# Two-layer hybrid attention, linear attention and MoE step: alternating level banks with output one head later, five more ada units on VectorE, a longer busy opening

## The chip, the cores and the metric

The kernel runs on one core of a Trainium2 chip. The metric is device time in microseconds of one execution. All data is float32. The engines that matter are PE (TensorE, matrix products), DVE (VectorE), ACT (ScalarE), POOL (GpSimd) and SP, which only issues DMAs.

## The reference

A step has two layers with the same structure. It handles two sequences of 128 tokens (s = 0: context, s = 1: latent tokens) of width 1024. Cut to what matters here:

```python
mod = silu(cond) @ w_ada + b_ada             # 6 x 1024 values per sequence: sh1, sc1, g1, sh2, sc2, g2
h = rmsnorm(x, norm1) * (1 + sc1) + sh1
q, k, v, gq, gk, gv, gg, lr_f, lr_b, ga, gb = split(h @ w_in)
o_attn = softmax(q k^T) v                    # 8 heads, 2 kv heads
o_gla, s_f, s_b = bidirectional_gla(gq, gk, gv, la_f, la_b, s0_f, s0_b)    # 4 heads
o_gla = rmsnorm(o_gla, gla_norm) * silu(gg)
merged = sigmoid(ga) * (o_attn @ w_pa) + sigmoid(gb) * (o_gla @ w_pb)
x = x + g1 * (merged @ w_out)
h2 = rmsnorm(x, norm2) * (1 + sc2) + sh2
x = x + g2 * grouped_moe(h2, ...)            # 16 experts, the best group of 4, top 2 in it
```

## The kernel before

**Weights.** All dense weights come through `ring`, six slots of 2 MB. `dense_order()` writes their order out by hand, and SP loads unit n when unit n - 6 has been used (`used(n)` names the semaphore). A unit is a piece of `w_ada` (12 per layer, `ada[0]` to `ada[11]`, 512 columns each), of `w_in` (five projections, then four of the gates ga and gb), `w_pa`, `w_pb` or one of two of `w_out`. After them the expert weights use the same slots, and three more (`more`, `mixer`).

**An ada unit** gives 4 x 128 values of `mod` for both sequences, in one of two ways. On PE: `ada_a` (L543, 8 products, 16 records in the trace) into bank 7, an ACT copy to the front half of `wide`, `ada_b` (L552, 4 transposes into bank 6), and two small DVE operations (`ada_bias`, L1456 and L1457). On DVE (`ada_blocks`, L1471): four blocks of two `SCALAR_TENSOR_TENSOR` over 1024 elements, one for each sequence, which read the ring slot and `cs_rows` (the silu of the condition in every partition) and write a throwaway product over all of `wide`. Before, units 4 to 7 of layer 0 go the second way (`VECTOR_ADA`), all others the first. The blocks stand at fixed places of DVE's program: 4 before the QK norm, 4 inside it, 2 before and 5 after the copy of gk, 1 after the first softmax. `cs_rows` is written by a POOL DMA from `cs_dram`, and lies over `qe`, `ke` and the front of `lpar` (the GLA state), which for this reason is loaded when the vector units are done.

**Opening** (layer 0). PE runs `WARM` products on zeros, then the first ada unit, the norm sum, ada unit 2, and half of the input projection (`first_half`, L667) while the other halves of the weights are still on their way; then ada units 1 and 3, and `second_half` (L676).

**Fills.** From the attention on, PE, ACT and DVE each call `fill(l)` at the same places of their programs; each call takes one entry of `fill_list(l)`: one of eight gate chunks (L563, 16 products), an ada unit, one of four `pa` chunks (L576, o_attn times w_pa, 8 products), or `HOLE`, nothing. The attention takes entries 0 to 6, all gates, to give PE work while DVE and ACT make the softmax (L1598 to L1604). The eighth gate and all else are taken in the linear attention, two entries a head. An ada unit that PE took is finished (`ada_b`, `ada_bias`) at the next fill. With the first `pa` entry ACT makes the sigmoids of the gates (L1124 to L1126, a table load before and after).

**Linear attention (GLA).** Head i of 8 (4 heads times 2 sequences) goes through: `gla_in` (PE L801, L807: decays into banks 0 and 1), the exponential (ACT L1232) into one of two halves of `ereg`, `qe` (DVE L1616) and `ke` (POOL L1948), `gla_levels` (PE L822, 8 products into banks 2 and 3), mask and sum (DVE L1634 twice, L1636) into `st`, `gla_out` (PE L845 and L850 or L847) and copies (ACT L1084, L1251). For the first four heads there is also `kst` (POOL L1953), its transpose (PE L832) and copy; for the last four `qin` (DVE L1620). POOL prepares `qz` for the next head (L1934) when `qe` is done. The order on PE for head i is: fill, `gla_in(i + 1)`, `gla_levels(i)`, `gla_keys(i)`, fill, `gla_out(i)`. `gla_levels(i)` waits until `st` of head i - 1 is made, since it writes the same banks.

**After it**: transposes (L872), `w_pb` (L890), `w_out` (L904), router, then the experts (L1015, L1027), whose weights are 100 MB a layer.

## Time and profile before

| | us |
|---|---|
| median of 3 runs | 1016.63 (1014.25 to 1022.54) |
| the profiled execution | 1020.26 |
| its span in the profile | 1018.1 |
| PE busy in the span | 961.9 (94%) |
| DVE busy | 383.7 (38%) |
| ACT busy | 237.6 (23%) |
| POOL busy | 99.9 (10%) |

A busy PE is not a PE at its peak, since its products are pipelined and their ends are modelled; start-to-start distances say more. In the rows, L543 is line 543 of the kernel before, "idle before <-X" is how long an engine stood still before an instruction and what released it, and PEclk is the granted share of the full clock of TensorE (1.00 is 2.4 GHz, 0.50 is 1.2 GHz).

### The profile page before, as it was taken

The page shows a single profiled execution, that of the slowest core. Times are in us where ns is not written, and L with a number is a line of the kernel's source. Part 1 is how long each engine was busy: PE and PEld are TensorE (multiplying, and loading weights), DVE is VectorE, ACT ScalarE, POOL GpSimd, SP SyncE. Part 2 cuts the span into 40 slices and gives each one's busy share as a digit, 9 for nine tenths or more (in the row PEclk, how much of TensorE's full clock was granted, in tenths as well). Part 3 has the DMA queues.
Part 4 walks back from the last instruction along what each step waited for, and adds up shares of the span by engine and source line. Part 5 has one row for each costly group of instructions (what it writes and reads, how often), then busy time and mean ns, then how long its engine had stood idle before and what let it go on. Part 6 is the DMA issues. An engine that isn't in the chain of part 4 may idle for free.

```text
span 1018.1 us, 13639 instructions
## 1 busy us (share of the span) xinstructions
PE 961.9 (94%) x4894; PEld 564.6 (55%) x4894; DVE 383.7 (38%) x1011; ACT 237.6 (23%) x521; POOL 99.9 (10%) x85
## 2 busy tenths in 40 slices
PE   6999999999989999999899999899899999999987
PEld 2348877777845443443344687777686444344333
DVE  4098612783261222222351421258535222222124
ACT  2113222521123222121140322352101232122111
POOL 0000003741100000000000000066310000000000
PEclk8999999999999999999999999999999999999999
DMA  9899552246989998999998533240877999989992
GB/s 392 372 364 420 209 203 102 109 192 269 416 346 411 418 422 361 423 421 421 426 427 352 194 110 139 83 166 6 336 296 284 402 407 423 421 365 421 421 421 100
DMA packets 37378, 317.48 MB, mean 312 GB/s; under 512 B 4280, under 2 KB 4432, under 8 KB 5328
## 3 DMA queue, kind: packets, MB, share of 16 engines
q1 hardware_dynamic: 36144, 311.28, 74.8%
q0 software_dynamic: 1184, 5.53, 1.4%
q8 instruction: 32, 0.52, 0.2%
q14 instruction: 18, 0.15, 0.0%
HBM read 314.93 MB, written 1.86 MB: 311 GB/s over the span
## 4 chain that ended last, share of the span: by engine, by line
PE 77%; DMA 13%; DVE 5%; ACT 3%; issue 2%; SPq 0%; ACTq 0%; DVEq 0%
PE ps L1015 18%; DMA ring<-w_gu 12%; PE ps L563 11%; PE ps L1027 7%; PE ps L709 7%; PE ps L904 5%; PE ps L973 3%; PE ps L890 3%; PE ps L727 3%; PE ps L822 2%; PE ps L576 2%; PE ps L667 2%; PE ps L543 1%; PE ps L988 1%; PE ps L676 1%
## 5 line engine op out<-in xcount | busy, mean ns | idle before, releaser
L1015 PE MATMUL ps<-ring,tmq 128*64 128x512 f32 x928 | 212.4, 598 | 18.3 <-DMA ring<-w_gu 14.8
L1015 PEld LDWEIGHTS ps<-ring,tmq 128*64 128x64 f32 x928 | 67.8, 138 | 143.5 <-issue 126.4
L563 PE MATMUL ps<-more,ring 128*128 128x256 f32 x512 | 114.3, 381 | 0.5 <-ACT more L1084 0.5
L1027 PE MATMUL ps<-ring,tmq 128*64 128x512 f32 x512 | 113.8, 596 | 0.0
L563 PEld LDWEIGHTS ps<-more,ring 128*128 128x128 f32 x512 | 96.1, 190 | 15.5 <-issue 2.5
L1848 DVE TENSOR_TENSOR tmq<-tmq,ps 128x256 f32<-128x256 f32 x32 | 13.5, 421 | 206.0 <-ACT tmq L1339 206.0
L1084 ACT ACTIVATE tmq<-ps 128x256 f32<-128x256 f32 (+3 forms) x124 | 55.6, 462 | 149.2 <-PE ps L709 62.8
L1027 PEld LDWEIGHTS ps<-ring,tmq 128*64 128x64 f32 x512 | 35.2, 137 | 65.7 <-issue 62.1
L709 PE MATMUL ps<-ring,more 128*128 128x512 f32 (+1 forms) x192 | 69.9, 523 | 0.0
L1859 DVE SCALAR_TENSOR_TENSOR x<-ps,mod,x 128x128 f32<-128x128 f32 x256 | 67.6, 342 | 1.9 <-PE ps L973 1.9
L1339 ACT ACTIVATE tmq<-ps 128x256 f32<-128x256 f32 x32 | 12.3, 383 | 226.1 <-PE ps L1015 226.1
L1835 DVE TENSOR_SCALAR tmq<-cst,st 128x64 f32<-128x64 f32 x72 | 17.8, 310 | 117.9 <-PE ps L960 117.2
L973 PE MATMUL ps<-tmq 128*128 128x256 f32 x256 | 58.7, 382 | 1.6 <-ACT tmq L1084 1.6
L904 PE MATMUL ps<-more,ring 128*128 128x256 f32 x256 | 56.4, 380 | 0.0
L709 PEld LDWEIGHTS ps<-ring,more 128*128 128x128 f32 x192 | 36.2, 190 | 32.9 <-issue 31.1
L904 PEld LDWEIGHTS ps<-more,ring 128*128 128x128 f32 x256 | 48.2, 190 | 7.1 <-issue 0.8
L973 PEld LDWEIGHTS ps<-tmq 128*128 128x128 f32 x256 | 47.3, 190 | 8.1 <-issue 2.0
L1084 ACT ACTIVATE tmq<-cst 128x512 f32 (+1 forms) x64 | 35.3, 623 | 47.9 <-issue 47.6
L1934 POOL TENSOR_TENSOR more<-tmq,cst 128x896 f32<-128x896 f32 x16 | 33.4, 2087 | 119.1 <-PE ps L758 109.4
L543 PE MATMUL ps<-ring,cs 128*32 128x512 f32 x320 | 40.3, 621 | 3.2 <-DMA ring<-w_ada 3.2
L1471 DVE SCALAR_TENSOR_TENSOR wide<-ring,mixer 128x1024 f32<-128x1024 f32 x32 | 39.2, 1224 | 7.4 <-DMA mixer<-cs_dram 6.4
L1948 POOL TENSOR_TENSOR mixer<-tmq,more 128x896 f32<-128x896 f32 x16 | 35.2, 2200 | 49.4 <-ACT more L1232 31.2
(254 smaller groups left out, 1031.1 us busy)
## 6 DMA issues: line engine op xcount, KB each, us to landing
ring<-w_gu SPq DMA_DIRECT2D x116, 1024.0 KB, 14.3
ring<-w_down SPq DMA_DIRECT2D x64, 1024.0 KB, 12.5
ring<-w_ada SPq DMA_DIRECT2D x24, 2048.0 KB, 11.3
ring<-w_in SPq DMA_DIRECT2D x14, 2048.0 KB, 17.4
ring<-w_out SPq DMA_DIRECT2D x4, 2048.0 KB, 10.8
more<-w_gu SPq DMA_DIRECT2D x8, 1024.0 KB, 14.6
cst<-consts SPq DMA_DIRECT2D x2, 2080.0 KB, 16.0
ring<-w_in SPq DMA_DIRECT2D x4, 1024.0 KB, 23.3
```

The lines of the kernel that those rows point to most:

```text
L543: mm = pe.matmul(ps[j:j + 32, 7, :], cs[:, k, :], w[:, k, :], start=k < 4, stop=k >= 4)
L563: mm = pe.matmul(ps[:, 5, i * NT:(i + 1) * NT], w[:, k, m * P:(m + 1) * P], h[:, k, :], start=k == 0, stop=k == KT - 1)
L709: mm = pe.matmul(ps[:, n % 4, 0:cols], h[:, k, (n % 2) * T:(n % 2) * T + T], w[:, k, 0:cols], start=i == 0, stop=i == KT - 1)
L904: mm = pe.matmul(ps[:, 4 + b % 4, (b // 4) * NT:(b // 4 + 1) * NT], w[:, k, (b % 4) * P:(b % 4 + 1) * P], sga[:, k, :], start=k == 0, stop ...
L973: mm = pe.matmul(ps[:, (4, 5, 7, 4)[f], j * NT:(j + 1) * NT], yy[:, k * P:(k + 1) * P], gwt, start=True, stop=True)
L1015: mm = pe.matmul(ps[r:r + SLOTS, half, :].rearrange("p (j n) -> p j n", j=2), hg[:, k, e, 0:SLOTS], gu_unit(l, kh, e, in_more)[:, part, :, ...
L1027: mm = pe.matmul(ps[r:r + SLOTS, 2 + n, :], at_[:, k, r:r + SLOTS], down_unit(l, k // 2)[:, e, k % 2, n * 512:(n + 1) * 512], start=k == 0 ...
L1084: return act.activation(out, in_, ACT.Copy, scale=scale)
L1471: link(dve.scalar_tensor_tensor(wide[:, :], w[:, i, :], 1.0, cs_rows[:, s, :], ALU.mult, ALU.mult, accum_out=mod[:, l, 4 * a + i, s:s + 1]))
L1859: ins = dve.scalar_tensor_tensor(x[:, k, c], ps[:, (4, 5, 7, 4)[f], j * NT + s * T:j * NT + (s + 1) * T], mod[:, l, 40 + k, s:s + 1], x[:, ...
L1934: pool.tensor_tensor(qz, q, C("side").rearrange("p (v t) -> p v t", t=T), ALU.mult).then_inc(g_qz, 1)
L1948: pool.tensor_tensor(halves(ke), kh.unsqueeze(1).to_broadcast([P, LEVELS, 2, HALF]), level_view(e), ALU.mult).then_inc(g_ke, 1)
```

## The change

- `VECTOR_ADA` becomes a list by layer: units 4 to 8 of layer 0 and 6 to 9 of layer 1 go to DVE. The blocks keep their places, now in both layers, and four more stand after the second softmax (used in layer 0 only, which has 20 blocks; layer 1 has 16). In layer 1 POOL loads `cs_rows` first, then the rest of `lparams` without the state, and the state when the vector units are done.
- A fill may now hold two entries. In layer 0, ada units 9 to 11 stand before gates 4 to 6, in the attention. In the GLA there is no ada unit left; `pa` is cut into eight halves, one a head, at the second fill. The ring order follows.
- Levels go to banks 2 and 3 for even heads, 6 and 7 for odd ones, and wait for `st` of two heads before. `gla_out(i - 1)` and `gla_keys(i - 1)` move into head i, after and before its levels. DVE makes `qe(i + 1)` before the mask of head i, and takes over `kst` from POOL; the carried query of the last four heads (`qin` before) has two buffers. The norm of the first sequence is cut into a beginning and an end, one head apart.
- The opening: `WARM` 10 instead of 6, and two times two products (`keep_busy`) around `ada_b` of the second ada unit; PE waits for `x` before its first ada unit.

```diff
...
 CS_ROWS = 1
 
...
+    return a in VECTOR_ADA[l]
 
...
 
 
...
 def fill_list(l):
-    gates = [("gate", c) for c in range(8)]
...
+    gates = [[("gate", c)] for c in range(8)]
     if l + 1 < LAYERS:
-        return gates + [ada[8], HOLE, pa[0], HOLE, pa[1], HOLE, ada[9], HOLE, pa[2], HOLE, pa[3], HOLE, ada[10], HOLE,
-                        ada[11]]
-    return gates + [ada[6], HOLE, pa[0], HOLE, pa[1], HOLE, ada[7], HOLE, pa[2], HOLE, pa[3], HOLE, ada[8], HOLE,
-                    ada[9]]
+        for c, a in zip(range(4, 7), range(VECTOR_ADA[l][-1] + 1, ADA)):
+            gates[c].insert(0, ("ada", a))
+    halves = [[("pa", i)] for i in range(8)]
+    return gates + [slot for half in halves for slot in (half, HOLE)]
...
-WARM = 6
+WARM = 10
+
+
+def fills_done(l):
+
+    return ADA * l + max([VECTOR_ADA[l][-1]] + [n for slot in fill_list(l) for kind, n in slot if kind == "ada"]) + 1
+
+
+def level_bank(i):
+
+    return 6 if i % 2 else 2
...
-        if l == 0:
-            out.append((l, "ada", VECTOR_ADA[0]))
+        vector = [(l, "ada", a) for a in VECTOR_ADA[l]]
...
-            if l == 0 and n == 2:
-                out.append((l, "ada", VECTOR_ADA[1]))
-        for kind, n in fill_list(l):
+            if n in (1, 3 if l else 2):
+                out.append(vector.pop(0))
+        for kind, n in itertools.chain(*fill_list(l)):
...
-                if l == 0 and n in (0, 2):
-                    out.append((l, "ada", VECTOR_ADA[2 + n // 2]))
+                for _ in range((1, len(vector))[n // 2] if n < 4 else 0):
+                    out.append(vector.pop(0))
...
+
+        carried = (qin[:, :], lrt[:, T:2 * T])
...
                 w = full(l, "ada", a)
-                if l == 0 and a == VECTOR_ADA[-1] + 1:
-                    pe.wait_ge(ada_mod, a)
+                if a == VECTOR_ADA[l][-1] + 1:
+                    pe.wait_ge(ada_mod, ada_turn(l, a))
...
-            def pa_chunk(l, m):
+            def pa_half(l, n):
 
                 w = full(l, "pa", 0)
-                if m == 0:
+                m, i = n // 2, n % 2
+                if n == 0:
                     pe.wait_ge(gate_exp, 8 * (l + 1))
-                else:
+                elif i == 0:
                     pe.wait_ge(pa_used, 4 * l + m)
...
+                for k in range(4):
+                    mm = pe.matmul(ps[:, 5, i * NT:(i + 1) * NT], w[:, k, n * P:(n + 1) * P], ot[:, k, :], start=k == 0,
+                                   stop=k == 3)
+                if i:
+                    mm.then_inc(pa_mm, 1)
...
             pe.wait_ge(dve_step, 1)
             for _ in range(WARM):
                 pe.matmul(ps[:, 3, :], wide[:, 0:P], wide[:, 0:512], start=True, stop=True)
+            def keep_busy(n):
+
+                for _ in range(n):
+                    pe.matmul(ps[:, 3, :], x[:, 0, 0:P], x[:, 0:2, :].rearrange("p k n -> p (k n)"), start=True, stop=True)
+
             pe.wait_ge(in_c, 16)
             pe.wait_ge(in_p, 16)
+            pe.wait_ge(in_x, 16)
...
                     ada_a(l, FIRST_ADA[1])
+                    keep_busy(2)
                     ada_b(l, FIRST_ADA[1])
+                    keep_busy(2)
                     first_half(0)
...
                 pe.wait_ge(att_o_copied, 4 * (l + 1))
                 pe.wait_ge(la_ready, 2 * (l + 1))
                 pe.wait_ge(in_late, HALVES_IN + 16 * (l + 1))
-                if l == 0:
-                    pe.wait_ge(in_lp, loaded(l, "state"))
...
                     n = 8 * l + i
                     pe.wait_ge(g_qe, n + 1)
                     pe.wait_ge(g_ke, n + 1)
-                    if i:
-                        pe.wait_ge(g_st, n)
+                    if i == 1:
+                        pe.wait_ge(ada_mod, fills_done(l))
+                    if i >= 2:
+                        pe.wait_ge(g_st, n - 1)
                     c = slice(s * T, (s + 1) * T)
                     for v in range(LEVELS + 1):
                         lhs, rhs = (ke[:, v, :], qe[:, v, :]) if v < LEVELS else (gqk[:, 1, hh, c], gqk[:, 0, hh, c])
-                        mm = pe.matmul(ps[:, 2 + v // 4, (v % 4) * T:(v % 4 + 1) * T], lhs, rhs, start=True, stop=True)
+                        mm = pe.matmul(ps[:, level_bank(i) + v // 4, (v % 4) * T:(v % 4 + 1) * T], lhs, rhs, start=True, stop=True)
...
+                    if i == GH:
+                        pe.wait_ge(in_lp, loaded(l, "state"))
                     if s:
-                        mm = pe.matmul(ps[:, 4, 256:384], qin[:, :], LP("state")[:, hh * DV:(hh + 1) * DV],
+                        mm = pe.matmul(ps[:, 4, 256:384], carried[i % 2], LP("state")[:, hh * DV:(hh + 1) * DV],
                                        start=False, stop=True)
...
@@ -855,11 +875,13 @@
                     fill(l)
                     if i < 7:
                         gla_in(i + 1)
+                    if 0 < i <= GH:
+                        gla_keys(i - 1)
                     gla_levels(i)
-                    if i < GH:
-                        gla_keys(i)
+                    if i:
+                        gla_out(i - 1)
                     fill(l)
-                    gla_out(i)
+                gla_out(7)
...
                     if i >= 2:
-                        act.wait_ge(g_qe, n - 1)
                         act.wait_ge(g_ke, n - 1)
-                        act.wait_ge(g_kst, 4 * l + min(i - 1, GH))
+                        act.wait_ge(g_st, n - 1)
...
                     fill(l)
                     if i < 7:
                         gla_in(i + 1)
-                    gla_kt(i)
+                    if i:
+                        gla_kt(i - 1)
+                        gla_out(i - 1)
+                    if i == GH + 1:
+                        inv_root(GLA_RMS, RSQ * l + 3)
                     fill(l)
-                    gla_out(i)
-                    if i == GH:
-                        inv_root(GLA_RMS, RSQ * l + 3)
-                fill(l)
+                gla_out(7)
...
-            blocks = [(a, i) for a in VECTOR_ADA for i in range(4)]
+            blocks = [[(a, i) for a in VECTOR_ADA[l] for i in range(4)] for l in range(LAYERS)]
 
             def ada_blocks(l, count):
 
-                for _ in range(count if l == 0 else 0):
-                    a, i = blocks.pop(0)
+                for a, i in blocks[l][:count]:
+                    blocks[l].remove((a, i))
                     n = PLACE[(l, "ada", a)]
                     w = ring[:, n % RING, :].rearrange("p (i k) -> p i k", i=4)
                     if i == 0:
+                        if l:
+                            dve.wait_ge(st_out, 16 * l)
...
-                    elif kind == "pa":
-                        merge_a(l, n)
+                    elif kind == "pa" and n % 2:
+                        merge_a(l, n // 2)
...
-                        if 2 * s + v == 0:
-                            ada_blocks(l, 1)
+                        ada_blocks(l, (1, 4, 0, 0)[2 * s + v])
...
-                    ins = dve.tensor_tensor(halves(qe), halves(qz), level_view(e), ALU.mult)
+                    dve.tensor_tensor(halves(qe), halves(qz), level_view(e), ALU.mult).then_inc(g_qe, 1)
                     if i >= GH:
-                        if i > GH:
-                            dve.wait_ge(g_o, n)
-                        ins = dve.tensor_tensor(qin[:, :].rearrange("p (h t) -> p h t", h=2),
-                                                gqk[:, 0, hh, s * T:(s + 1) * T].rearrange("p (h t) -> p h t", h=2),
-                                                edge_view(e), ALU.mult)
-                    ins.then_inc(g_qe, 1)
+                        if i > GH + 1:
+                            dve.wait_ge(g_o, n - 1)
+                        dve.tensor_tensor(carried[i % 2].rearrange("p (h t) -> p h t", h=2),
+                                          gqk[:, 0, hh, s * T:(s + 1) * T].rearrange("p (h t) -> p h t", h=2),
+                                          edge_view(e), ALU.mult)
+
+                def gla_kst(i):
+                    e = ereg[:, i % 2, :]
+                    if i or l:
+                        dve.wait_ge(g_kt, 4 * l + i)
+                    dve.tensor_tensor(kst[:, :].rearrange("p (h t) -> p h t", h=2),
+                                      gqk[:, 1, i, 0:T].rearrange("p (h t) -> p h t", h=2), edge_view(e),
+                                      ALU.mult).then_inc(g_kst, 1)
 
...
-                    if i:
-                        dve.wait_ge(g_o, n)
...
                     link(ins)
-                    dve.tensor_reduce(st[:, :], ps[:, 2:4, :].rearrange("p a (v t) -> p t (a v)", v=4), AX,
+                    if i:
+                        dve.wait_ge(g_o, n)
+                    dve.tensor_reduce(st[:, :], ps[:, b:b + 2, :].rearrange("p a (v t) -> p t (a v)", v=4), AX,
                                       ALU.add).then_inc(g_st, 1)
...
-                def gla_norm(s):
+                def gla_norm_begin(s):
                     dve.wait_ge(g_o_copied, 8 * l + 4 * s + 4)
                     dve.wait_ge(gg_ready, l + 1)
-                    inv_rms(GLA_RMS, DV, sm[:, 64 + GH * s:64 + GH * (s + 1)], RSQ * l + 3 + s)
+                    if s:
+                        dve.wait_ge(g_normed, 2 * l + 1)
+                    inv_rms_begin(GLA_RMS, DV, sm[:, 64 + GH * s:64 + GH * (s + 1)])
+
+                def gla_norm_end(s):
+                    inv_rms_end(GLA_RMS, RSQ * l + 3 + s)
...
                 gla_q(0)
+                gla_kst(0)
                 for i in range(8):
                     fill(l)
-                    gla_mask(i)
                     if i < 7:
                         gla_q(i + 1)
+                    gla_mask(i)
+                    if i + 1 < GH:
+                        gla_kst(i + 1)
                     fill(l)
                     if i == GH:
-                        gla_norm(0)
-                    if i in (GH + 1, GH + 2):
+                        gla_norm_begin(0)
+                    if i == GH + 1:
+                        gla_norm_end(0)
+                    if i > GH + 1:
                         for hh in range(2):
-                            ins = gla_scale(0, 2 * (i - GH - 1) + hh)
-                        if i == GH + 2:
+                            ins = gla_scale(0, 2 * (i - GH - 2) + hh)
+                        if i == 7:
                             ins.then_inc(g_normed, 1)
                 fill(l)
-                gla_norm(1)
+                gla_norm_begin(1)
+                gla_norm_end(1)
                 for hh in range(GH):
...
-                late = 0 if l else GH * DV
+                late = GH * DV
...
-                    pool.wait_ge(in_lp, loaded(l, "cs_rows"))
+                pool.dma_start(cs_rows, cs_dram.rearrange("s k p -> s (k p)").unsqueeze(0).to_broadcast([P, S, D])
+                               ).then_inc(in_lp, 16)
+                pool.wait_ge(in_lp, loaded(l, "cs_rows"))
                 pool.dma_start(lpar[:, late:LW], lparams[l, :, late:LW]).then_inc(in_lp, 16)
...
-                if l == 0:
-                    pool.wait_ge(ada_mod, VECTOR_ADA[-1] + 1)
-                    pool.dma_start(lpar[:, 0:late], lparams[l, :, 0:late]).then_inc(in_lp, 16)
+                pool.wait_ge(ada_mod, ada_turn(l, VECTOR_ADA[l][-1]) + 1)
+                pool.dma_start(lpar[:, 0:late], lparams[l, :, 0:late]).then_inc(in_lp, 16)
...
-                    if i < GH:
-                        if i or l:
-                            pool.wait_ge(g_kt, 4 * l + i)
-                        pool.tensor_tensor(kst[:, :].rearrange("p (h t) -> p h t", h=2), kh, edge_view(e),
-                                           ALU.mult).then_inc(g_kst, 1)
                     if i < 7:
                         queries(i + 1)
...
```

## Rows read from the trace of the kernel before

**Rows 1.** Windows from:to in us: length, each engine's busy time (count), PEclk, DMA share, GB/s.
```profile
164.60:228.10 63.50, 62.48 (x467) 45.54 (x468) 43.58 (x54) 23.17 (x49) 36.79 (x20) 1.00 0.35 137
297.50:518.30 220.80, 211.60 (x1009) 90.22 (x1010) 57.77 (x207) 48.34 (x100) 0.00 (x0) 1.00 0.99 412
660.20:723.80 63.60, 62.56 (x467) 45.61 (x468) 43.58 (x54) 23.21 (x49) 36.79 (x20) 1.00 0.35 135
```
**Rows 2.** Timeline of PE, one head of layer 0: start, duration, line, operation, count.
```profile
196.42 1.83 PE L822 MATMUL ps<-mixer 128*128 128x128 f32 x14
198.51 1.92 PE L543 MATMUL ps<-ring,cs 128*32 128x512 f32 x16
...
201.15 0.66 PE L552 MATMUL ps<-cst,wide 128*128 128x128 f32 x4
201.74 0.88 PE L801 MATMUL ps<-cst,mixer 64*64 64x384 f32 x8
...
203.13 1.83 PE L822 MATMUL ps<-mixer 128*128 128x128 f32 x14
...
205.02 3.62 PE L576 MATMUL ps<-more,ring 128*128 128x256 f32 x16
```
**Rows 3.** Timeline of PE in the opening.
```profile
1.47 7.23 PE L638 MATMUL ps<-wide 128*128 128x512 f32 x12 [1.47 <-DVE wide L1497]
11.95 3.61 PE L543 MATMUL ps<-ring,cs 128*32 128x512 f32 x16 [3.25 <-DMA ring<-w_ada]
...
22.96 10.13 PE L667 MATMUL ps<-ring,more 128*128 128x512 f32 x16 [1.62 <-DVE more L1447]
...
42.08 3.60 PE L667 MATMUL ps<-ring,more 128*128 128x512 f32 x8
```
**Rows 4.** One window of the opening, columns as in rows 1.
```profile
12.00:14.00 2.00, 2.00 (x12) 0.66 (x16) 0.00 (x0) 0.00 (x0) 0.00 (x0) 0.50 0.94 401
```
**Rows 5.** The chain of waits, first gate of layer 0 after the transposes of sequence 1.
```profile
132.88 3.24 PE ps L563 x15
```
**Rows 6.** Groups of DVE instructions by line: count, busy us, mean ns, idle before.
```profile
L1471 DVE SCALAR_TENSOR_TENSOR wide<-ring,mixer 128x1024 f32<-128x1024 f32 x32 | 39.2, 1224 | 7.4 <-DMA mixer<-cs_dram 6.4
L1634 DVE TENSOR_TENSOR ps<-ps,cst 128x512 f32<-128x512 f32 x32 | 22.0, 697 | 23.7 <-PE ps L822 22.2
L1636 DVE TENSOR_REDUCE st<-ps 128x128 f32<-128x1024 f32 x16 | 19.6, 1224 | 0.5
```
**Rows 7.** Timeline of DVE: end of the second softmax, layer 0.
```profile
125.85 0.69 DVE L1604 TENSOR_TENSOR more<-more,sm 128x512 f32<-128x512 f32 x1
```
**Rows 8.** Timeline of DVE, layer 1: four places where it waits.
```profile
555.78 1.49 DVE L1530 TENSOR_TENSOR more<-tmq 128x1280 f32<-128x1280 f32 x1 [14.03 <-ACT tmq L1084]
...
569.82 0.18 DVE L1396 TENSOR_TENSOR sm<-sm 128x20 f32<-128x20 f32 x1 [10.81 <-ACT sm L1090]
...
592.89 2.80 DVE L1580 COPY tmq<-ps 64x512 f32<-64x512 f32 x4 [5.81 <-PE ps L727]
608.80 0.69 DVE L1598 TENSOR_REDUCE sm<-ps 128x4 f32<-128x512 f32 x1 [13.12 <-PE ps L758]
```
**Rows 9.** Timeline of ACT in the GLA: an exponential; the sigmoids' first and last instruction.
```profile
174.58 1.02 ACT L1232 ACTIVATE more<-ps 128x1024 f32<-128x1024 f32 x1 [0.81 <-PE ps L807]
...
183.67 1.28 ACT L1124 ACT_TABLE_LOAD   x1
...
188.69 1.28 ACT L1126 ACT_TABLE_LOAD   x1
```
**Rows 10.** Timeline of DVE in the GLA of layer 0.
```profile
167.22 1.09 DVE L1616 TENSOR_TENSOR mixer<-more 128x896 f32<-128x896 f32 x1 [7.63 <-ACT more L1232]
...
180.12 1.97 DVE L1457 TENSOR_TENSOR mod<-mod,par 128x8 f32<-128x8 f32 x1
```
**Rows 11.** Timeline of POOL in the same stretch.
```profile
167.27 2.98 POOL L1948 TENSOR_TENSOR mixer<-tmq,more 128x896 f32<-128x896 f32 x1 [11.15 <-ACT more L1232]
...
179.99 2.08 POOL L1934 TENSOR_TENSOR more<-tmq,cst 128x896 f32<-128x896 f32 x1
```

45 lines of the change are left out of this document (19 added, 26 removed).

## The prediction

> **What bounds the kernel now.** I read the page first: PE is busy for 961.9 of 1018.1 us, the other engines for 38% and less. That share says little of where a change pays, so the windows by stage come next. In the linear attention (GLA) of either layer, from its first product to the last output, PE is busy for 62.5 of 63.5 us [rows 1], while DVE is busy for 43.6 and POOL for 36.8. The stage is bound by the amount of PE work in it, not by the round trip through DVE: a head that has an ada unit takes 6.71 us from one `gla_levels` to the next (196.42 to 203.13), and product follows product [rows 2]. In the expert stage the DMA engines are busy 99% of the time at 412 GB/s, with PE at 211.6 of 220.8 us [rows 1]. Its transfers are let go by ring slots that PE frees from `w_pb` on, so the whole stage moves with the end of the mixer, and what the mixer gains or loses is passed on one for one. In the opening PE stands still before its first ada unit and before `first_half` [rows 3], and runs at 0.50 of its clock after the first of these [rows 4].
>
> **Alternating banks and the later output** take away waits that PE hardly has: about 1 us a layer [rows 1]. By themselves I cost them at nothing. They are needed as cover once the ada fills, which now hide DVE's work between levels and output, are gone.
>
> **Ada units off PE.** One unit costs PE 1.92 us for the products and 0.59 for the transposes (201.15 to 201.74), 2.5 together [rows 2]. Each GLA had four of them, so 10.0 us of PE work leave it. What stays of a head is 6.71 - 2.5 = 4.2 us, plus half a `pa` chunk, 3.62 / 2 = 1.8 [rows 2]: a period of 6.0 us, some 0.2 less in the last heads without `keys`. Two things eat into it. The sigmoids hold ACT for 6.3 us (183.67 to 189.97) [rows 9]; they now start with the first half of `pa` in head 0, one head earlier. From the end of `gla_in(1)` ACT makes an exponential (1.0), the sigmoids, the next exponential (1.0) and the key copy (0.3), 8.6 us, and `gla_out(0)` waits for that; PE has levels, half a chunk, `gla_in(2)` and levels meanwhile, 2.0 + 1.8 + 1.4 + 2.1 = 7.3. That is 1.3 us. The last head has no follower to hide its mask and sum (2 x 0.70 + 1.22 us [rows 6]) except one output and half a chunk, 2.4 us; with DVE a little behind I take 0.9. So the GLA shortens by 10.0 - 1.3 - 0.9 = 7.8 us a layer, **-15.6** in both.
>
> **Three of these units come back in layer 0.** Units 9 to 11 now stand before gates 4 to 6. There a gate chunk of 7 us already outlasts the softmax of DVE and ACT, so nothing hides them: 3 x 2.5 = **+7.5**. In layer 0 the real saving is one unit.
>
> **The vector blocks, layer 0.** A block is two instructions of 1.224 us [rows 6], with gaps 2.5 us. Blocks 17 to 20 start when the second softmax is normed, at 126.5 [rows 7], and end 10.1 us later, at 136.7. But `ada_a(9)` waits for exactly that, and it is now the first thing PE does at 132.88, where the gate chunk started at once before [rows 5]. Behind it on PE are that gate, the scores of sequence 1 and all that follows; ACT and DVE wait with them. PE stands still for **+3.9** us. It goes on slower as well: after 3.25 us without work in the opening its first ada unit took 3.61 us instead of 1.92 [rows 2, 3], at a granted clock of 0.50, which is the 1.2 GHz level [rows 4]. I take the same loss again, **+1.7**; the bounds are nothing and the 3.2 us that `first_half` lost. If the opening makes PE earlier, these blocks move along, since they hang on scores that PE makes.
>
> **The vector blocks, layer 1.** 4, 4, 2 and 5 blocks (10.1, 10.1, 5.1 and 12.7 us) fall into waits of 14.0, 10.8, 5.8 and 13.1 us [rows 8], the last after the softmax into another. All fit, by 0.4 us at the closest, so I cost them at nothing; without the cover it would be 38 us. They need `cs_rows`, a 1 MB transfer from POOL's queue, before 541.6, and it is issued when layer 0 ends, near 520; the remaining `lparams` come behind it and are wanted at 555. The state comes after the last block and is wanted in head 4, some 60 us later. A ring slot with a vector unit is held until DVE is through, but the input projection takes 13.7 us a unit for 5 us of DMA. If this slips, I bound it at 5 us.
>
> **DVE and POOL in the GLA.** `kst` leaves POOL for DVE (0.3 us in four heads). Per head DVE has `qe` 1.1, two masks 1.4, the sum 1.2, a small product 0.3, half a merge 0.35, and in the last heads norm and scaling, 0.6: 4.4 to 5.0 of 6.0 us, so it fits as long as POOL does not hold it up (rival 1).
>
> **The opening.** The four extra warm products are 8 records of 0.43 us, 3.4 us: 8.70 + 3.4 = 12.1, and the weights are there at 11.95 [rows 3]. So PE no longer idles before its first ada unit and should keep the full clock through it. The second unit's 2.1 MB come 5.2 us after the first at 401 GB/s [rows 4], near 17.1; it then takes 1.9, two `keep_busy` products 1.7, `ada_b` 0.6 and two more 1.7, and `first_half` starts near 22.9, as before (22.96). Its 16 records then take 2 x 3.44 = 6.9 us at the rate of the later ones (42.08) instead of 10.13 [rows 3]. That is 3.2, with 0.2 for the start: **-3.4**. Bounds: -4.5 if the start gains a microsecond too, +1.7 if two products merely stand in the way.
>
> **Sum:** -3.4 + 7.5 + 3.9 + 1.7 - 15.6 = -5.9 us. Against the profiled execution, 1020.3, that is 1014.4. This execution lies 3.6 above the median of the runs, 1016.6, so I forecast **1010.7 us**, 0.6% faster. A measurement of this kernel can tell about 1% (10 us) from no change.
>
> **Rival 1, slower: POOL gets between two DVE operations in every late head.** `qe(i + 1)` and POOL's `ke(i + 1)` now start on the same event. The trace shows what this does: with `qe` at 167.22, `ke` at 167.27 takes 2.98 us instead of its 2.1, so it waited; and a DVE product of 8 elements took 1.97 us beside a POOL product that ran from 179.99 to 182.07 [rows 10, 11]. In heads 4 to 7 `qe` has the carried query right behind it, on two SBUF operands, and `ke` already waits. If POOL goes first, the loop from one `st` to the next is exponential 1.0, `qe` 1.1, `ke` 2.1, carried query 0.3, masks 1.4, sum 1.2 and 0.2 of handovers: 7.3 us against 5.9 of PE work. It decides from the point where the loop without `ke`, 5.2 us, no longer fits. Price: 1.4 us in four heads of two layers, 11 us, or **1021.8 us**. No row shows two such DVE operations in a row with POOL waiting, so for is only the 2.98, against is that DVE starts its next operation before the last has ended. The Trainium skill, SBUF — State Buffer, section "SBUF: two separate sides", says that GpSimd and a VectorE operation with two SBUF inputs take a shared port pair as an exclusive lock, and the loser is blocked for the whole instruction. By that the two rows above are explained, and both outcomes remain open, since the page does not say who is served after a release.
>
> **Rival 2: the opening does not do what it says.** The clock falls in spite of the products, or they delay `ada_b`. Then -3.4 becomes about 0: **1014.1 us**. [...]
>
> **Rival 3: PE does not stand still in layer 0's attention**, because the blocks are done by then or PE comes later. Without the 3.9 and 1.7 it is **1005.1 us**. I see no row for it except that the wait is computed, not seen.
>
> **Chances.** The forecast with its terms 0.43 (own range 1007 to 1014.5), rival 1, in full or in part, 0.30, rival 2 0.15, rival 3 0.12. Rival 1 together with a late transfer in layer 1 reaches 1027. The range that leaves out no more than 2 in 10 is 1004.5 to 1023.5. Faster by over 1% means below 1006.5, which needs rival 3 or two good ends at once: 0.14. Slower by over 1% needs rival 1 and another miss: 0.05. Within 1%: 0.81.
>
> **What would show it.** In the profile after: the stretch from the first GLA product to the last output at 55.7 us in both layers (61 under rival 1, with PE waiting for `st` and DVE's carried query beginning 2 us after `qe`); PE idle for about 3.9 us before L543 in layer 0's attention, released by DVE's bias of unit 8; 16 records of `first_half` in 6.9 us; in layer 1 the gates at the same distance from the start of the layer as before. The forecast is wrong if either GLA stays above 60 us, or if the gates of layer 1 come later by microseconds.

## The result and the profile after

| | before | after |
|---|---|---|
| median of 5 runs each, us | 1016.63 (1014.12 to 1022.54) | 1025.61 (1024.49 to 1027.93) |
| profiled execution, us | 1020.26 | 1026.16 |
| its span, us | 1018.1 | 1024.4 |

The ratio of the times is **1.0078 (95% interval 1.005 to 1.0105)**: the change makes the kernel 0.8% slower. Forecast were 1010.7 us, 0.6% faster, with a range of 1004.5 to 1023.5 that doesn't hold the time. Six more runs on another chip gave 1.0077 (1.0046 to 1.0108).

To find the difference I cut both profiled executions at the same events of PE: first `gla_in`, last GLA output, first expert product, last expert product.

| stretch | before | after | difference | forecast |
|---|---|---|---|---|
| start to first `gla_in` of layer 0 | 164.6 | 174.6 | +10.0 (opening -3.3, attention +13.3) | +9.7 |
| GLA layer 0 | 63.4 | 60.65 | **-2.8** | -7.8 |
| tail and router, layer 0 | 69.5 | 72.1 | **+2.6** | 0 |
| experts, layer 0 | 215.9 | 215.6 | -0.3 | 0 |
| layer 1 up to its GLA | 146.8 | 146.8 | 0 | 0 |
| GLA layer 1 | 63.4 | 60.3 | **-3.2** | -7.8 |
| tail and router, layer 1 | 66.8 | 67.5 | +0.7 | 0 |
| experts, layer 1 | 217.6 | 216.5 | -1.1 | 0 |
| sum | | | +6.0 | -5.9 |

The windows of the changed kernel that answer to rows 1 (start and end, length, then busy time of PE, PEld, DVE, ACT, POOL, PEclk, DMA share, GB/s), with the window of layer 0's attention on top:

```profile
93.90:174.60 80.70, 72.31 (x395) 56.07 (x395) 38.05 (x67) 18.76 (x54) 2.63 (x2) 0.96 0.68 274
174.60:235.20 60.60, 53.92 (x392) 41.53 (x392) 48.14 (x53) 20.23 (x44) 38.17 (x16) 1.00 0.13 43
669.80:730.00 60.20, 53.53 (x388) 41.13 (x388) 46.21 (x51) 20.23 (x44) 38.15 (x16) 1.00 0.12 42
```

PE's work in the GLA fell as forecast, from 62.5 to 53.9 and 53.5 us, but the stretch did not follow: PE now stands still for 6.7 us in it, where it stood for 1.0 before. The waits of PE in the GLA of layer 0 (line, what it waited for: total us, times, longest) say for what:

```profile
PE ps L863 <- ACT lrt L1106: 3.1, 2, 1.6
PE ps L863 <- DVE st L1673: 1.7, 3, 0.6
PE ps L840 <- DVE mixer L1645: 1.6, 1, 1.6
```

Here "ACT lrt" is ACT's copy of the transposed `kst`, and "DVE mixer" is `qe`.

In the opening, the changed kernel's PE timeline shows all of rows 3 mended: the first ada unit at full clock (1.92 us, not 3.61), and `first_half` in 7.10 us, not 10.13. It starts at 22.67, as it did at 22.96.

```profile
12.15 1.92 PE L553 MATMUL ps<-ring,cs 128*32 128x512 f32 x16
...
22.67 7.10 PE L683 MATMUL ps<-ring,more 128*128 128x512 f32 x16
```

In layer 0's attention the standstill is there, 3.98 us, and everything behind it is slow until the clock is back: the ada unit takes 3.64 us, the gate chunk 7.82 instead of 7.07. The PE timeline, and then that of DVE at the end of the 20th and last block of the vector units (its last two instructions before PE goes on):

```profile
133.55 3.64 PE L553 MATMUL ps<-ring,cs 128*32 128x512 f32 x16 [3.98 <-issue]
137.12 7.82 PE L573 MATMUL ps<-more,ring 128*128 128x256 f32 x32
```
```profile
133.16 0.08 DVE L1502 DVE_READ_ACCUMULATOR wide<-ring,mixer 128x1 f32 x1
133.28 0.17 DVE L1506 TENSOR_TENSOR mod<-mod,par 128x8 f32<-128x8 f32 x1
```

PE goes on 0.1 us after the bias of unit 8. That the row says "issue" for the wait and not DVE is no evidence against it; the experiment `gate_first` settles it.

### The profile page after: what moved, and what is told of

It reads as the page before. It is cut to its first block, busy times and chain, and to the rows that moved or that the text cites. A ratio compares the mean times of both kernels' runs of the same rounds, so it can differ in the third digit from the quotient of the medians.

```text
span 1024.4 us, 13524 instructions
## 1 busy us (share of the span) xinstructions
PE 957.4 (93%) x4810; PEld 561.8 (55%) x4810; DVE 441.1 (43%) x1094; ACT 233.9 (23%) x516; POOL 103.7 (10%) x79
## 4 chain that ended last, share of the span: by engine, by line
PE 73%; DMA 13%; DVE 6%; ACT 4%; issue 3%; SPq 0%; ACTq 0%; DVEq 0%
PE ps L1037 18%; DMA ring<-w_gu 12%; PE ps L573 11%; PE ps L1049 7%; PE ps L727 7%; PE ps L926 5%; PE ps L995 3%; PE ps L912 3%; PE ps L745 3%; PE ps L553 2%; PE ps L1010 1%; DMA ring<-w_ada 1%; PE ps L683 1%; PE ps L692 1%; DVE st L1673 1%
## 5 line engine op out<-in xcount | busy, mean ns | idle before, releaser
L1037 PEld LDWEIGHTS ps<-ring,tmq 128*64 128x64 f32 x928 | 67.5, 137 | 142.5 <-issue 125.1
L1502 DVE SCALAR_TENSOR_TENSOR wide<-ring,mixer 128x1024 f32<-128x1024 f32 x72 | 88.1, 1224 | 11.9 <-DMA mixer<-cs_dram 9.8
L1995 POOL TENSOR_TENSOR mixer<-tmq,more 128x896 f32<-128x896 f32 x16 | 46.2, 2890 | 50.2 <-ACT more L1252 37.7
L553 PE MATMUL ps<-ring,cs 128*32 128x512 f32 x240 | 32.7, 660 | 5.1 <-issue 4.0
```

Of the source, the lines that this page charges most:

```text
L553: mm = pe.matmul(ps[j:j + 32, 7, :], cs[:, k, :], w[:, k, :], start=k < 4, stop=k >= 4)
L1037: mm = pe.matmul(ps[r:r + SLOTS, half, :].rearrange("p (j n) -> p j n", j=2), hg[:, k, e, 0:SLOTS], gu_unit(l, kh, e, in_more)[:, part, :, ...
L1502: link(dve.scalar_tensor_tensor(wide[:, :], w[:, i, :], 1.0, cs_rows[:, s, :], ALU.mult, ALU.mult, accum_out=mod[:, l, 4 * a + i, s:s + 1]))
L1995: pool.tensor_tensor(halves(ke), kh.unsqueeze(1).to_broadcast([P, LEVELS, 2, HALF]), level_view(e), ALU.mult).then_inc(g_ke, 1)
```

## The experiments

Theory: the GLA does not get shorter because POOL's `ke` runs between `qe` and the carried query on DVE (rival 1 of the prediction), and the rest of the loss is layer 0's attention, as forecast. Against it stand: DVE simply has too much to do in a head; the carried product is slow by itself; the sigmoids are the whole loss.

### Who runs between two DVE operations

DVE of the changed kernel in heads 4 to 6 and POOL in head 4 (start, duration, line, operation):

```profile
205.30 1.09 DVE L1645 TENSOR_TENSOR mixer<-more 128x896 f32<-128x896 f32 x1 [0.38 <-PE ps L840]
206.31 2.17 DVE L1649 TENSOR_TENSOR qin<-tmq,more 128x128 f32<-128x128 f32 x1
208.41 1.28 DVE L1669 TENSOR_TENSOR ps<-ps,cst 128x512 f32<-128x512 f32 x2
...
212.12 1.09 DVE L1645 TENSOR_TENSOR mixer<-more 128x896 f32<-128x896 f32 x1 [0.58 <-ACT more L1252]
213.13 2.17 DVE L1649 TENSOR_TENSOR lrt<-tmq,more 128x128 f32<-128x128 f32 x1
...
218.94 1.09 DVE L1645 TENSOR_TENSOR mixer<-more 128x896 f32<-128x896 f32 x1 [1.10 <-ACT more L1252]
```
```profile
205.31 3.02 POOL L1995 TENSOR_TENSOR mixer<-tmq,more 128x896 f32<-128x896 f32 x1 [0.54 <-PE ps L840]
```

`ke` is issued 0.01 us after `qe`, and takes 3.02 us instead of 2.1: it waits out `qe` and then runs. The carried query, issued at 206.31 for 128 elements, ends at 208.48, right behind `ke` (208.33). One head takes 6.82 us (212.12 to 218.94). In head 7 POOL is first by 0.01 us, and `qe` itself waits:

```profile
225.81 3.01 DVE L1645 TENSOR_TENSOR mixer<-more 128x896 f32<-128x896 f32 x1 [0.17 <-ACT more L1252]
```
```profile
225.80 2.08 POOL L1995 TENSOR_TENSOR mixer<-tmq,more 128x896 f32<-128x896 f32 x1 [1.74 <-ACT more L1252]
```

Before, the carried query took 0.28 us, since POOL's `ke` was over when `qe` began (`ke` 198.62 to 200.72 and `qin` at 201.59 in its trace). `kst`, which DVE took over from POOL for the first four heads, meets the same lock: 2.17, 1.77, 0.85 and 1.51 us (at 178.26, 190.55, 197.80 and 203.42) where the prediction had 0.3. PE does not wait for it there.

**`pool_after`**: POOL waits for both DVE operations in the late heads.

```diff
-  dve.tensor_tensor(qe ...).then_inc(g_qe, 1)
+  ins = dve.tensor_tensor(qe ...)
   if i >= GH:
-      dve.tensor_tensor(carried ...)
+      ins = dve.tensor_tensor(carried ...)
+  ins.then_inc(g_qe, 1)
...
   pool.wait_ge(g_exp, n + 1)
+  if i >= GH:
+      pool.wait_ge(g_qe, n + 1)
```

> The changed kernel with POOL's ke of heads 4 to 7 made to wait until DVE is through with qe and the carried query. Theory A (the lock between POOL and DVE's pair): carried query 0.3 us right behind qe; ke takes 2.1 us and DVE's next operations with two SBUF operands may be held instead; the GLA stretches fall to 56 to 58 us. Theory B (the amount of work on DVE): 60 to 61 us as in the changed kernel. What PE waits for in the last heads tells which: under A neither st nor the mixer.

Measured: 1019.93 us, one run. The GLA takes **56.6 us in layer 0 and 56.3 in layer 1**, 4.0 less in each than in the changed kernel. DVE and POOL at the same place:

```profile
205.36 1.09 DVE L1645 TENSOR_TENSOR mixer<-more 128x896 f32<-128x896 f32 x1 [0.39 <-PE ps L840]
206.37 0.29 DVE L1649 TENSOR_TENSOR qin<-tmq,more 128x128 f32<-128x128 f32 x1
...
211.13 1.09 DVE L1645 TENSOR_TENSOR mixer<-more 128x896 f32<-128x896 f32 x1 [1.42 <-PE ps L840]
...
214.81 1.91 DVE L1419 TENSOR_SCALAR sm<-sm 128x4 f32<-128x4 f32 x1
216.91 1.09 DVE L1645 TENSOR_TENSOR mixer<-more 128x896 f32<-128x896 f32 x1 [0.19 <-PE ps L840]
```
```profile
206.79 2.08 POOL L1998 TENSOR_TENSOR mixer<-tmq,more 128x896 f32<-128x896 f32 x1 [1.97 <-DVE qin L1649]
```

The carried query takes 0.29 us, `ke` 2.08, a head 5.78 us (211.13 to 216.91): the period of PE's work. `ke` starts 1.5 us later and ends 0.5 us later than in the changed kernel (208.87 and not 208.33), and yet the loop is shorter, since DVE is through with the carried query 1.8 us earlier and its masks (1.29 us for two, as without POOL beside them) run beside `ke`; they have one operand in PSUM and one in SBUF and are not held. So DVE had time enough, and theory B falls. The waits of PE in this stretch:

```profile
PE ps L840 <- issue: 2.2, 3, 1.8
PE ps L863 <- ACT lrt L1106: 1.5, 1, 1.5
```

PE waits no more for `st` or `qe`. What is left is the first output behind the sigmoids (1.5 us; the forecast had 1.3) and 1.8 us ahead of the last levels (226.52). The row says "issue", but `ke` of the last head ended at 226.42. Part of this delay is the new order, and part is the lock once more: a small product of the norm, which takes 0.15 us in the changed kernel, runs beside POOL's scaled query (220.38 to 222.46), so that `qe` starts at 222.92 though its exponential was ready at 221.80.

```profile
221.18 1.31 DVE L1425 TENSOR_TENSOR sm<-sm 128x4 f32<-128x4 f32 x1
```

The second wait for ACT's `lrt`, 1.6 us before the output of head 3 (212.40), is gone; ACT's exponential ahead of that copy waited for DVE's `st` (211.06, and 209.24 in `pool_after`).

**`carried_late`**: the carried query of head i+1 behind the mask and sum of head i.

```diff
...
   gla_mask(i)
   if i + 1 < GH:
       gla_kst(i + 1)
+  elif i < 7:
+      gla_carried(i + 1)
```

> The changed kernel with one thing moved: on DVE the product carried query (L1649) of head i+1 stands behind head i's mask and sum instead of right behind qe(i+1). Theory A (POOL's waiting ke gets between two back-to-back DVE operations): the carried query no longer takes 2.17 us but 0.3 in heads 5 to 7, qe keeps 1.1, and the stretch from the first GLA product to the last output falls from 60.6 us to 55.5 to 57 in layer 0 and from 60.2 likewise in layer 1; with the tails unchanged that is 7 to 10 us less for the run, some 1017. Theory B (DVE has too much work in a head, or the small product is slow by itself): the stretches stay at 60 to 61 us and the run at 1025. Theory C (only the first output's wait for the sigmoids and a slower tail are at fault): less than 1 us a layer.

Measured: 1021.14 us (10 runs), ratio to the kernel before 1.0016 (0.9997 to 1.0036); GLA 58.4 and 57.9 us, half of the way. The small product met the lock at its new place:

```profile
208.26 1.22 DVE L1678 TENSOR_REDUCE st<-ps 128x128 f32<-128x1024 f32 x1
209.41 1.76 DVE L1654 TENSOR_TENSOR qin<-tmq,more 128x128 f32<-128x128 f32 x1
...
211.69 2.90 DVE L1645 TENSOR_TENSOR mixer<-more 128x896 f32<-128x896 f32 x1
```

At 209.41 POOL's next scaled query (208.92 to 211.02) was running, and because DVE was behind, `ke` then came ahead of `qe` (2.90 us). I had expected 55.5 to 57: moving the victim doesn't take the lock away, ordering the two engines does.

**`carried_first`**: the two DVE operations swapped.

```diff
+  if i >= GH:
+      dve.tensor_tensor(carried ...)
   dve.tensor_tensor(qe ...).then_inc(g_qe, 1)
-  if i >= GH:
-      dve.tensor_tensor(carried ...)
```

> The changed kernel with the order of the two DVE operations swapped in heads 4 to 7: the small carried query first, qe behind it. Theory A (after the first operation of a pair the waiting ke of POOL goes next, whatever the operations are): the carried query takes 0.3 us and qe, now second, about 3.2 us (2.1 of it ke's), ke about 2.1 to 2.4; the GLA stretches stay at 60 to 61.5 us. Theory B (the small product with its strided operands is slow by itself): it stays at 2.2 us, qe at 1.1.

Measured: 1028.25 us, one run; GLA 60.6 and 60.2.

```profile
205.83 0.29 DVE L1648 TENSOR_TENSOR qin<-tmq,more 128x128 f32<-128x128 f32 x1 [0.39 <-PE ps L840]
206.04 2.97 DVE L1651 TENSOR_TENSOR mixer<-more 128x896 f32<-128x896 f32 x1
```
```profile
205.84 2.22 POOL L1995 TENSOR_TENSOR mixer<-tmq,more 128x896 f32<-128x896 f32 x1 [0.55 <-PE ps L840]
```

In heads 4 to 6 whichever of the two stands second pays for `ke` (in head 7 `ke` was first again, and the carried query, now first on DVE, took 2.21 us). The small product with its strided operands is not slow by itself. This settles what the prediction had to leave open: **a POOL operation that waits is served between two DVE operations that follow each other without a gap.** The Trainium skill, SBUF — State Buffer, section "SBUF: two separate sides", says that whichever starts first has the shared port pair for its whole instruction and the other blocks; the rows agree (3.02 us of `ke` is 1.0 of `qe` and 2.1 of its own), and add that DVE doesn't keep the pair for its next operation.

### The standstill in layer 0's attention

**`gate_first`**: the same units in the same slots, behind the gate chunk.

```diff
-  gates[c].insert(0, ("ada", a))
+  gates[c].append(("ada", a))
```

> The changed kernel with the fills of layer 0's attention in the other order: gate chunk first, ada unit behind it. Theory A (PE stands still because ada_a(9) waits for the vector block of unit 8, and comes back at half clock): the 3.98 us standstill before the ada products goes, the gate chunk after it takes 7.0 us and not 7.8, the ada products 1.9 and not 3.6, and layer 0's attention stretch falls from 80.7 to 74.5 to 76 us; the run is about 5 to 6 us shorter. Theory B (DVE is what bounds the attention here, so the stall appears at the scores or their products one step later): 78 to 81 us, PE waiting elsewhere. Everything before that stretch stays the same.

Measured: 1020.62 us (10 runs), ratio to before 1.0003 (0.9984 to 1.0022), where the changed kernel has 1.0077 and 1.0078. The attention stretch starts at 93.9, as in the changed kernel, and ends at 168.1: 74.2 us, 6.5 less.

```profile
129.48 0.27 PE L763 MATMUL ps<-cst,mixer 128*128 128x128 f32 x1
129.59 7.07 PE L573 MATMUL ps<-more,ring 128*128 128x256 f32 x32
136.59 1.92 PE L553 MATMUL ps<-ring,cs 128*32 128x512 f32 x16
```

No idle time, full clock. The standstill and the slow clock behind it are confirmed as causes; together they are worth 6.5 us, where the prediction had 3.9 + 1.7 = 5.6. The standstill had its size (3.98), the clock cost 2.5: 1.7 in the ada unit and 0.75 in the gate chunk. Theory B, that DVE would hold PE one step later, falls.

### Both repairs, the banks, and the tail

**`best`**: `gate_first` and `pool_after` together.

> The changed kernel with both repairs: the gate chunk ahead of the ada unit in layer 0's attention, and POOL's ke of heads 4 to 7 held until DVE is through with qe and the carried query. If the two losses are independent, as the theory has it, the savings add: 6.3 us in the attention and 4.3 and 3.9 us in the two GLA stretches, 14.5 us below the changed kernel, so some 5 us (0.5%) below the kernel before, ratio 0.993 to 0.997. Rival: what PE gains is given back where the expert stage's weights have to arrive, so that its transfers become the bound; then the ratio stays at 0.998 to 1.002 and the expert stages are longer than 220.5 and 226.8 us.

Measured: 1012.03 us (12 runs), **ratio to before 0.9931 (0.9909 to 0.9953)**. The savings add: the ratio is 1.5% below the changed kernel's 1.0077, and 14.5 us were expected. The GLA is at 56.65 and 56.25 us, the attention as in `gate_first`. The rival, that the expert stages take the gain back, falls by the ratio. In this trace the one of layer 0 is 2.7 us longer than in the changed kernel (218.3 against 215.6), the one of layer 1 as long (216.4 against 216.5); `gate_first` and `pool_after` have 215.9 and 215.5 in layer 0.

**`best_one_bank`**: `best` with the levels of all heads in one pair of banks.

```diff
-  return 6 if i % 2 else 2
+  return 2
...
-  if i >= 2:
-      pe.wait_ge(g_st, n - 1)
+  if i:
+      pe.wait_ge(g_st, n)
```

> The kernel with both repairs, but with the levels of all heads in one pair of banks: levels of head i wait until DVE has summed head i-1. The prediction costed the alternating banks at nothing by themselves and said that they are cover once the ada fills are gone. Theory A (they are needed): without them PE waits for the sum in each head, exponential to sum 5 to 6 us against 5.8 of PE work, plus 2 us of levels that no longer overlap: 1 to 2 us a head, 8 to 14 us a layer. Theory B (the fill between hides the sum anyway): under 1 us a layer.

Measured: 1015.86 us (10 runs), 0.9948 (0.9924 to 0.9972). GLA 57.83 and 57.44 us. In layer 0 PE waits for the sum of the head before:

```profile
PE ps L840 <- DVE st L1674: 3.5, 5, 1.9
PE ps L863 <- ACT lrt L1106: 0.9, 1, 0.9
```

So the alternating banks are worth 1.2 us a layer net in the stretches (the intervals of the two ratios overlap), between my two expectations: DVE's sum is done 0.2 to 0.5 us after PE asks for it, and 1.9 in the worst head. Costing them at nothing was nearly right.

**`best_tail`**: the tail of layer 0 was the second surprise. In the changed kernel PE stands still for 1.61 us between its two blocks of transposes, and comes back at half clock (`ada` products 3.6 us). The variant puts that ada unit, which nothing holds back, into the gap.

```diff
...
   for s in range(S):
+      if s:
+          for w in pre[:1]:
+              ada_a(*w)
       pe.wait_ge(g_normed, 2 * l + s + 1)
...
-  for w in pre[:1]:
-      ada_a(*w)
```

> The same, and in layer 0's tail PE makes the first ada unit of the next layer between the two blocks of transposes instead of behind them (L894, L553). Theory A (the tail of layer 0 got 2.8 us slower because PE's granted clock falls after it stood still for 0.9 and 1.8 us): the second block takes 0.6 us and not 1.1, the ada products 1.9 and not 3.6, the gap of 1.8 us is filled; the stretch from the last output to the first expert product falls from 72.2 to 67 to 69.5 us, 3 to 5 us for the run. Theory B (the clock falls whatever stands there, by what went before in the GLA): the ada products take 3.6 us in their new place, and about 1.8 us are won, from the gap alone.

Measured: 1011.35 us (9 runs), 0.9915 (0.9888 to 0.9943), and in a second measurement (`opening_pair_new`, below) 1009.42 us (6 runs), **0.9888 (0.9853 to 0.9923)**. PE in `best`, then in `best_tail`:

```profile
227.94 1.12 PE L894 MATMUL ps<-cst,tmq 128*128 128x128 f32 x4 [1.83 <-DVE tmq L1689]
...
229.38 2.76 PE L553 MATMUL ps<-ring,cs 128*32 128x512 f32 x13
```
```profile
225.48 0.63 PE L898 MATMUL ps<-cst,tmq 128*128 128x128 f32 x4 [0.88 <-DVE tmq L1690]
226.04 1.92 PE L553 MATMUL ps<-ring,cs 128*32 128x512 f32 x16
227.94 0.66 PE L898 MATMUL ps<-cst,tmq 128*128 128x128 f32 x4
```

The gap of 1.83 us is filled and the clock stays up; the tail takes 68.3 us instead of 71.0. All four traces with the filled tail have 68.3 to 68.5 us; the eight others of the changed GLA have 70.7 to 72.5, each with a fall of the clock in the gap or behind it. Theory B, that the clock falls whatever stands there, falls itself.

For the whole run the expected 3 to 5 us did not show beside `best`: 1011.35 against 1012.03 us on one chip, with intervals that overlap. In the two traces layer 0 ends its experts at 513.6 and 513.9 us, since the expert stage took 220.7 us in `best_tail` and 218.3 in `best`. 1.9 us of that are slower products (108.8 against 106.9 us, the group of the next section), the rest is not taken apart. What the filled tail is worth over many runs is not resolved.

### What the opening is worth, and the scatter

**`before_opening`**: the kernel before with the new opening alone.

```diff
-WARM = 6
+WARM = 10
...
+  pe.wait_ge(in_x, 16)
...
+  keep_busy(2)
   ada_b(l, FIRST_ADA[1])
+  keep_busy(2)
   first_half(0)
```

> The kernel before with the changed opening alone: ten warm products instead of six, the wait for x ahead of them, and two pairs of busy products around the second ada unit's transposes. Theory A (the opening gains 3.3 us and everything behind it moves up): first_half ends 3.3 us earlier, its 16 records take 7.1 us and not 10.1, the run is 3.3 us shorter, ratio 0.9967. Theory B (what is gained is taken back later, since the layer's next weights come by the DMA queue and not by PE): the stretch behind the opening gets longer by as much and the ratio is 0.999 to 1.001.

Measured: 1019.49 us (12 runs), ratio 1.001 (0.9982 to 1.0038). The first `gla_in` stands at 161.2 us, 3.4 earlier than before, and the span of the profiled execution is 4.4 shorter, but over the runs nothing is gained. `before_again` and `opening_again` are for this.

> The kernel before once more, for a second trace of its opening. Its runs lie between 1014 and 1024 us with mean granted clocks between 0.985 and 0.997, and the changed opening alone did not shorten them (ratio 1.001) though its trace is 3.4 us ahead when the linear attention begins. Theory A (the loss in the old opening differs between executions): here first_half takes less than 10.1 us or starts before 22.96. Theory B (the opening is always as in the first trace, and the gain is given back or hidden by differences further on): the same 10.1 us, 22.96 and 164.6 us within 0.3.

> The kernel before with the changed opening alone, once more. Theory B above: the linear attention begins at 161.2 us again, and the rest of the run differs by some microseconds from its first trace, in the expert stages or in places at half clock. Theory A: the beginning at 161.2 us differs too.

The kernel before, a second time (1016.28 us): its first `gla_in` is at 163.1 us and not 164.6, since after the same late first ada unit `first_half` took 8.66 us and not 10.13 (rows 3).

```profile
11.95 3.24 PE L543 MATMUL ps<-ring,cs 128*32 128x512 f32 x16 [3.04 <-DMA ring<-w_ada]
...
22.92 8.66 PE L667 MATMUL ps<-ring,more 128*128 128x512 f32 x16 [1.62 <-DVE more L1447]
```

The new opening, a second time (1021.23 us): 161.2 us again, but 5.4 us more behind it than in its first trace. So the gain is 1.9 to 3.4 us in the traces: the loss in the old opening differs between executions, and the gain is also hidden by what comes behind. It stands against differences of the same size elsewhere. Where they come from shows in the group of expert products of layer 0 (count | busy us, mean ns of one | idle before), in the kernel before, its opening variant, and that variant a second time:

```profile
L1015 PE MATMUL ps<-ring,tmq 128*64 128x512 f32 x464 | 105.4, 594 | 9.2 <-DMA ring<-w_gu 7.4 <-issue 1.9
```
```profile
L1023 PE MATMUL ps<-ring,tmq 128*64 128x512 f32 x464 | 107.1, 602 | 8.5 <-DMA ring<-w_gu 6.6 <-issue 1.9
```
```profile
L1023 PE MATMUL ps<-ring,tmq 128*64 128x512 f32 x464 | 108.8, 610 | 7.5 <-DMA ring<-w_gu 5.6 <-issue 1.9
```

The same products take 105.4, 107.1 or 108.8 us, in steps of 1.7. The granted clock of the stage is 1.00, 0.99 and 0.98. I read a step as one fall of the clock to its lower level. How many a run has is not the program's alone: over 80 executions of the kernel before, on four chips, the time is 1019.4 us on average, from 1014 to 1024, and it follows the mean granted clock (0.997 in the fastest, 0.986 in the slowest).

**`best_old_opening`**, **`opening_pair_new`**, **`opening_pair_old`**, **`opening_third`**: the kernel with both repairs and the filled tail, with either opening, and the opening alone once more.

> The kernel with both repairs and the filled tail, but with the old opening (six warm products, no busy products). If the opening is worth the 3.3 us of its stretch, the time is 3.3 us above that of the kernel with the new one, ratio to the kernel before 0.9948 against 0.9915. If it is worth nothing over many runs, as the run with the opening alone says, 0.991 to 0.992.

> Both repairs, filled tail, new opening, for a comparison on one chip with the same kernel that has the old opening. If the 3.3 us of the opening's stretch reach the end of the run: a ratio to the kernel before 0.003 lower than its partner's, some 0.9895 against 0.9925. If they do not: equal within 0.0015.

> The partner with the old opening: 3.3 us more than the kernel with the new one if the opening is worth what its stretch shows, the same within 1.5 us if what it gains is lost again behind it.

> The kernel before with the changed opening alone, in five more rounds: ratio 0.9967 if its 3.3 us reach the end (two traces have the linear attention at 161.2 us, the kernel before at 164.6 and 163.1, so 1.9 to 3.4 us), 1.000 to 1.001 if it is as in the first twelve runs.

| | runs | median us | ratio to before |
|---|---|---|---|
| repaired, old opening (`best_old_opening`) | 7 | 1012.99 | 0.9915 (0.9885 to 0.9945) |
| repaired, new opening, other chip (`opening_pair_new`) | 6 | 1009.42 | 0.9888 (0.9853 to 0.9923) |
| repaired, old opening, same chip as the row above (`opening_pair_old`) | 6 | 1011.82 | 0.9905 (0.987 to 0.994) |
| opening alone, second measurement, same chip (`opening_third`) | 12 | 1016.79 | 0.9972 (0.995 to 0.9994) |

The first row equals the ratio of `best_tail` with the new opening, 0.9915, as expected if the opening is worth nothing. On one chip the pair then differs by 2.4 us in favour of the new opening, with intervals that overlap, and the opening alone now gains 0.28%. The first 1.001 and this 0.9972 overlap at 0.998 to 0.999. The opening is worth something between nothing and 3 us over many runs; that all 3.3 arrive is neither shown nor excluded.

**`after_again`**: the changed kernel, unedited, on a second chip.

> The changed kernel itself, in as many rounds as its variants and beside them. The first measurement gave a ratio of 1.0078 (1.005 to 1.0105) from five runs against five. The stages say 6.3 us for the two profiled executions, 1.0062. I expect 1.0055 to 1.0085; GLA stretches again 60.6 and 60.2 us, 3.98 us of standstill before ada_a(9).

Measured: 1027.75 us (6 runs), 1.0077 (1.0046 to 1.0108). GLA 60.65 and 60.3 us again, 3.99 us of standstill, all as expected; tail of layer 0 again 72.1.

## Why the prediction was wrong

**The step that failed is the GLA term, "the GLA shortens by 10.0 - 1.3 - 0.9 = 7.8 us a layer".** It measured 2.8 and 3.2. I took DVE to fit "as long as POOL does not hold it up" and put 0.30 on the case that it does. It does, in every late head of both layers. With POOL held back the stretch is 56.6 and 56.3 us against my 55.7, so the rest of the term was sound to a microsecond. PE's busy time fell by 8.6 and 9.0 us against 10.0 worked out from starts, and the sigmoids cost 1.45 us (forecast 1.3). The last head cost 1.8 and not 0.9, and not by the wait I priced: PE waits there for `ke` ahead of the levels, and not for mask and sum. `kst` on DVE, put at 0.3 us, took up to 2.17, at no cost to PE. POOL's part is 4.0 us a layer, below the 5.6 that rival 1 gave it, because its loop of 6.8 us was shorter than the 7.3 I worked out. The prediction had said that it is wrong if either GLA stays above 60 us; both did.

**Point by point.**
- Opening -3.4: -3.3 in the profiled pair, by the mechanism named (full clock through the first unit, `first_half` in 7.1 us against the forecast 6.9). Over many runs it is smaller and not resolved, since the old opening doesn't always lose as much as in rows 3.
- Three ada units in layer 0's attention +7.5, standstill +3.9, clock behind it +1.7, together 13.1: measured 13.3, which is 6.8, 4.0 and 2.5. The standstill is right; that the sum is met so closely is luck, since the units cost 0.7 less and the clock 0.8 more. `gate_first` gives 6.5 back for a swap of two list entries, and leaves the 6.8 of the units.
- Blocks of layer 1 at nothing: right. That layer takes 146.8 us up to its GLA, to the tenth what it took before.
- Alternating banks at nothing: 1.2 us a layer as cover, as `best_one_bank` shows; already inside the GLA figure.
- The tails at nothing: wrong by 3.3 us in this pair, though not all of it is the change (below).
- Expert stages at nothing: -0.3 and -1.1 in this pair, inside the scatter of the kernel before alone (215.3 and 217.6 us for layer 1 in its two traces).

**The tails.** The granted clock in the 10 us behind the last output of layer 0, in the changed kernel and in the second trace of the kernel before:

```profile
235.25:245.25 10.00, 7.57 (x33) 4.11 (x34) 2.62 (x15) 2.94 (x9) 3.52 (x8) 0.66 0.59 211
```
```profile
226.52:236.52 10.00, 7.82 (x41) 4.50 (x41) 2.56 (x15) 2.89 (x9) 3.52 (x8) 0.83 1.01 428
```

In the five traces with the old GLA it is 1.00 in two, with a tail of 69.5 us, and 0.83 in three, with 71.2. In the eight of the new GLA without the filled gap it is never 1.00: 0.83 in three, with 70.7 to 71.2 us, and 0.66 in five, with 71.8 to 72.5. So the tail goes by the clock, which falls more often and stays low for longer behind the new GLA, and the pair of the table had the old kernel in one of its good executions. In layer 1 the old GLA has tails from 65.2 to 68.0 us, so +0.7 is inside the scatter. Before, an ada unit stood around the last output, as the one of [rows 2] in its head; I had not asked what PE meets there once it is gone.

**The sum.** The span moved by +6.3 against a forecast of -5.9, 12.2 us: 9.6 of it in the GLA (-15.6 against -6.0), 3.3 in the tails, less 1.4 in the expert stages; 0.3 is the stretch ahead of the first GLA, and the rest lies behind the last expert product. The time of the profiled executions moved by 5.9, so it is 11.8 above the 1014.4 worked out for it. The other 3.1 us to the median lie in the scaling: the profiled execution of before lay 3.6 above its median, that of after 0.5 above its own. Against the mean of 80 executions, 1019.4, the one profiled was an ordinary one, and the median of the first three runs, 1016.6, was low. Taking 3.6 us off for that was a step of its own, and it pushed the whole range down.

**Rival 1 was the case**, with its mechanism, at 8 us instead of 11. Its own time of 1021.8 lies inside the range; what lifted the result past 1023.5 are the tails (3.3) and the scaling (3.1) on top of it. Its sign in the rows was right but for one detail: the carried query starts 1.0 us after `qe` and not 2, and is held once it has started. The chance of 0.05 for slower by over 1% did no harm, since 0.8% is inside 1%.

## What to carry to other kernels

Two engines that are let go by the same event and share a lock need an order between them: put the wait on the one that leaves the loop alone, even if it then starts later (here `ke` ended 0.5 us later, DVE's chain 1.8 us earlier). When work is taken off the bounding engine, go through the stage as if that work had been cover, and look at each place where the engine now meets a wait, its last unit above all. A unit that depends on a late producer belongs behind, not ahead of, the work in its slot that depends on nothing.

## What the runs showed of the hardware

- A waiting POOL operation gets in between two DVE operations with two SBUF operands that follow each other without a gap: 0.28 becomes 2.17 us (changed kernel, the carried query and `kst` of head 0), 1.09 becomes 2.97 (`carried_first`).
- When both are released together it is a matter of 0.01 to 0.04 us who is first: in heads 4 to 6 of the changed kernel `qe` keeps 1.09 us and `ke` takes 2.98 to 3.02, in head 7 `ke` is first (225.80) and `qe` takes 3.01.
- A DVE TENSOR_SCALAR over 4 elements with a single tensor operand is held as well: in `pool_after` 1.91 us at 214.81 beside POOL's operation that ran from 214.61 to 216.69, against 0.16 in the changed kernel at 217.68, with POOL idle. Masks (PSUM and one SBUF operand) and sums over PSUM were not.
- TensorE's granted clock falls after short standstills in some executions and not in others: behind a gap of 1.83 us in the tail of layer 0 it stayed at full in the first trace of the kernel before and fell in the second (1.82 us there), and the tail was 1.7 us longer. The times of this one program lie up to 10 us apart, and the longer ones have the lower mean clock.
